# Fourteen products whose sum nobody reads, behind the sums of five norms of a two-model kernel

## The reference, cut to what matters

```python
def rms_norm(x, g):
    xf = x.astype(jnp.float32)
    y = xf * lax.rsqrt(jnp.mean(xf * xf, axis=-1, keepdims=True) + EPS)
    return (y * g.astype(jnp.float32)).astype(x.dtype)

for l in range(DEPTH):                                   # DEPTH = 2
    ...
    h = rms_norm(x, norm1_g[l]) * (1.0 + sc1) + sh1
    proj = h @ w_in[l]
    ...
    x = x + g1 * mixed
    h = rms_norm(x, norm2_g[l]) * (1.0 + sc2) + sh2
    u = causal_dwconv(h @ w_up[l], ffn_conv_w[l], ffn_conv_b[l])
    ...
    x = x + g2 * ((jax.nn.silu(gate) * val) @ w_down[l])

# second block, once
hn = rms_norm_2(x, norm_g);  proj = hn @ w_in            # then attention of three kinds, y @ w_out
hn = rms_norm_2(x, norm_g);  x + jnp.square(jax.nn.relu(hn @ w_up)) @ w_down
```

## Time and profile before

| | |
|---|---|
| median of three runs | 1836.68 us (1833.19 to 1836.99) |
| profiled execution, its own time | 1837.2 us |
| its span, first to last instruction | 1835.6 us |
| PE busy | 1691.9 us (92%) |
| POOL busy | 1255.8 us (68%) |
| DVE, ACT busy | 872.4 us (48%), 861.5 us (47%) |
| share of the last-ended chain on PE | 76% |
| mean granted clock of PE | 0.935 of full |

### The profile page before, as it was taken

One profiled execution on the slowest core, in us unless ns is written; L12 is line 12 of the kernel. 1 busy time (PEld: TensorE's weight loads), 2 busy tenths in 40 slices (PEclk: granted clock), 3 DMA queues, 4 the chain that ended last, 5 costly groups with the idle time before them and its releaser, 6 DMA issues.

```text
span 1835.6 us, 33961 instructions
## 1 busy us (share of the span) xinstructions
PE 1691.9 (92%) x13290; PEld 1639.6 (89%) x13290; DVE 872.4 (48%) x1774; ACT 861.5 (47%) x1411; POOL 1255.8 (68%) x948
## 2 busy tenths in 40 slices
PE   8999998989989999899998989979999986579999
PEld 8998997989889999899997989879999984479999
DVE  2457576466445643567665475434431354532200
ACT  2254444554346653464454554346654442335532
POOL 1467965656569999567965656658988790048886
PEclk8699999989889999999998989989999896589999
DMA  7245753446436667446753557446656650035664
GB/s 271 85 150 165 247 181 121 162 160 219 137 128 210 229 200 250 122 145 184 253 167 121 162 176 232 121 122 178 184 173 186 212 171 15 1 92 172 184 184 128
DMA packets 85518, 302.75 MB, mean 165 GB/s; under 512 B 9840, under 2 KB 12528, under 8 KB 85104
## 3 DMA queue, kind: packets, MB, share of 16 engines
q1 hardware_dynamic: 85360, 300.59, 51.2%
HBM read 299.50 MB, written 1.05 MB: 164 GB/s over the span
## 4 chain that ended last, share of the span: by engine, by line
PE 76%; DVE 10%; POOL 4%; issue 3%; ACT 3%; DVEq 2%; DMA 1%; SPq 0%; ACTq 0%; POOLq 0%
PE gemm_bank L1441 62%; POOL w_lo L390 4%; PE turn_bank L1548 2%; PE turn_bank L1518 1%; PE score_bank L1518 1%; ACT w_hi L408 1%; PE outp_bank L1536 1%; DVE rstd_row L766 1%; DVE conv L746 1%; PE outp_bank L1695 1%; DMA ada_w<-in_w_ada 1%; DVE idx_score L746 1%; PE score_bank L1441 1%; PE outp_bank L1583 1%; DVE probs L933 1%
## 5 line engine op out<-in xcount | busy, mean ns | idle before, releaser
L390 POOL TENSOR_TENSOR w_lo<-w_raw,w_hi 128x512 fp32r<-128x512 f32 x944 | 1255.6, 1358 | 568.3 <-ACT w_hi L408 566.3
L408 ACT ACTIVATE w_hi<-w_raw 128x1024 fp32r<-128x1024 f32 x472 | 492.6, 1046 | 700.5 <-PE gemm_bank L1441 673.2
L1441 PE MATMUL gemm_bank<-h_hi,w_hi 128*128 128x256 f32 x2112 | 613.6, 291 | 41.4 <-DVE h_lo L746 16.2
L1441 PE MATMUL gemm_bank<-h_lo,w_hi 128*128 128x256 f32 x2112 | 604.9, 286 | 0.0
L1441 PE MATMUL gemm_bank<-h_hi,w_lo 128*128 128x256 f32 x2112 | 604.6, 286 | 0.0
L1441 PEld LDWEIGHTS gemm_bank<-h_hi,w_hi 128*128 128x128 f32 x2112 | 412.9, 196 | 52.3 <-DVE h_lo L746 17.0
L1441 PEld LDWEIGHTS gemm_bank<-h_lo,w_hi 128*128 128x128 f32 x2112 | 413.2, 196 | 0.1
L1441 PEld LDWEIGHTS gemm_bank<-h_hi,w_lo 128*128 128x128 f32 x2112 | 412.7, 195 | 0.0
L746 DVE SCALAR_TENSOR_TENSOR conv<-gemm_bank,params_sb,conv 128x255 f32<-128x255 f32 (+1 forms) x320 | 139.5, 477 | 186.6 <-ACT conv L681 130.5
L1441 PE MATMUL gemm_bank<-w_hi,h_hi 128*128 128x256 f32 (+2 forms) x704 | 207.8, 295 | 18.4 <-DVE h_lo L746 8.0
L1441 PE MATMUL gemm_bank<-w_lo,h_hi 128*128 128x256 f32 (+2 forms) x704 | 202.7, 288 | 0.0
(11 more groups left out here) (284 smaller groups left out, 2268.9 us busy)
## 6 DMA issues: line engine op xcount, KB each, us to landing
w_raw<-in_stream SPq DMA_DIRECT2D x458, 512.0 KB, 3.7
ada_w<-in_w_ada SPq DMA_DIRECT2D x80, 512.0 KB, 4.8
ada_first<-in_w_ada SPq DMA_DIRECT2D x16, 512.0 KB, 10.6
w_raw<-in_stream SPq DMA_DIRECT2D x8, 256.0 KB, 2.7
alibi_sb<-in_alibi SPq DMA_DIRECT2D x1, 1920.0 KB, 7.3
rows_sb<-in_rows SPq DMA_DIRECT2D x1, 1536.0 KB, 10.6
residual<-in_x_t SPq DMA_DIRECT2D x1, 1024.0 KB, 7.4
out_x<-residual SPq DMA_DIRECT2D x4, 256.0 KB, 4.4
```

Of the source, the lines that this page charges most:

```text
L390: ins = nc.gpsimd.tensor_tensor(w_lo[:, s, e], w_raw[:, s, e], w_hi[:, s, e].bitcast(f32), ALU.subtract)
L408: A(w_hi[:, s, 0:n], w_raw[:, s, 0:n], ACT.Copy).then_inc(hi_ready, 1)
L1441: ins = M(o, a, b, start=first and i == 0, stop=last and i == len(passes) - 1, skip_group_check=True)
```

## The change

A function `filler` is added to PE's program. It multiplies the ones with the first 256 columns of the constants 14 times, each time into the same columns of `S.bank[0]`, and nothing reads them. square_sum_x calls it behind its own products, after the semaphore increment that releases DVE, in every norm but the first. Nothing else changes, on PE or on any other engine.

```diff
+            def filler():
+                for i in range(14):
+                    M(S.bank[0][:, 0:SEQ], ones[:, 0:P], cst[:, 0:SEQ], start=True, stop=True)
+
             def square_sum_x(l, which):
                 i = (O_N2 if which else O_N1) if l < DEPTH else (O2_N2 if which else O2_N1)
                 b, out = take(O, l, i)
...
                         pe.wait_ge(sq_ready, (2 * l + which) * 4 + kt // 2 + 1)
                     ins = M(out[:, 0:SEQ], ones[:, 0:P], sq[:, kt, :], start=kt == 0, stop=kt == KT - 1)
                 ins.then_inc(o_full, 1)
+                if l or which:
+                    filler()
```

## The result

The changed kernel took 1824.11 us (median of seven runs, 1816.74 to 1828.25), and the kernel before 1833.19 us in its seven runs (1827.9 to 1837.8; the three shown ahead of the prediction are among them). The ratio is 0.9945, with a 95% interval of 0.9925 to 0.9966. On the 1836.68 us from which the forecast counted, that is 10.1 us (6.2 to 13.8) less. I had forecast 5.5.

What follows compares the result with a forecast made beforehand. PE was taken to bound the kernel, by standing idle and by working at half clock. Of 10.8 us behind five norms, falls take 5.3, leaving 5.5: 1836.68 - 5.5 = 1831.2 us, range 1825.5 to 1835.0.

Steps and rivals of the forecast that it cites:

- What the half clock cost: Behind the five norms' waits for h, PE works at 0.50 for 24.21 us; at most 10.8 us can be won.
- The length of the filler, 6.1 us, and its cover: In the five norms' waits for h, 28 passes take 6.1 us and leave 2.0 or 1.7 us of idle time.
- Whether what lies behind keeps pace: Behind the norms' restarts, weights and h arrive in time for faster products; loss 0, bound 1 us in all.
- The price of a fall, 1.5 us: Behind a shortened wait at a norm, losing the clock costs 1.5 us, against 2.2 us on average now.
- The number of falls, 3.5 of five: At the five norms' shortened waits, the clock falls in 3.5, which takes 5.3 us from the gain.
- seven idle times: PE idle times of 1.51 to 2.75 us in the trace, begun at full clock; five were followed by half clock.
- The advice of the Trainium skill: Rival at the norms: shortened waits are harmless, the clock holds, 10.8 us won, 1825.9 us; chance 0.25.

## Why the prediction was wrong

- **What the half clock cost, 10.8 us.** Right. With 17 products the same stretches held 90 products more, 10.9 us, and the time fell by 12.8 us (8.4 to 17.1).
- **The length of the filler, 6.1 us, and its cover.** Right. It ended 6.0 us behind the sums, the idle time left was 2.05, 1.97, 2.05, 1.74 and 1.75 us, and the restart didn't move.
- **Whether what lies behind keeps pace.** Right at the norms: 48 products took 5.85 us at four restarts.
- **The price of a fall, 1.5 us.** Right: 36 products instead of 48.
- **The number of falls, 3.5 of five.** This is the step that failed. It was 4 of 15. The sum with 1.3 falls is 10.8 - 2.0 = 8.8 us, within the interval of what was measured. I had pooled seven idle times because their lengths were near, and had taken the share of falls among them for a chance that holds at any wait. The runs show no such chance. Longer idle times lost the clock more often behind the filler (none of 30 restarts with 0.4 to 0.8 us, 4 of 15 with 1.73 to 2.05, 4 of 5 with 2.60 to 2.91), but elsewhere the idle time of 1.51 us in the first two layers' attention was followed by half clock in 13 of 28 cases, and that of 2.35 to 2.40 us for the convolution in 18 of 28, counted over the profiles of all runs here. At one place and one length the cases sort themselves by another quantity, how long before the idle time the clock had last risen:

| idle time, between the same two instructions | clock had last risen | what followed |
|---|---|---|
| 1.51 us, attention | 59.9 to 60.8 us ahead | held in 15 of 15 |
| 1.51 us, attention | 58.7 to 59.6 us ahead | fell in 9 of 9 |
| 2.35 to 2.40 us, convolution | 74.0 to 74.5 us ahead | held in 5 of 5 |
| 2.35 to 2.40 us, convolution | 74.8 to 75.9 us ahead | fell in 14 of 14 |

The other 13 cases had risen at quite other times. Two cases of the attention in the second layer, each with its 1.51 us and then the 3.5 us behind it, first with 7 products in the norms (last risen 60.2 us ahead), then with the one-column products (59.6 us ahead):

```profile
1140.34 0.43 PE L1589 MATMUL outp_bank<-qkv,probsT 128*128 128x64 f32 x2 [1.51 <-DVE probsT L906]
1140.34:1143.84 3.50, 3.25 (x27) 3.01 (x28) 1.36 (x4) 1.44 (x2) 0.73 (x1) 1.00 0.02 5
```

```profile
1144.17 0.45 PE L1589 MATMUL outp_bank<-qkv,probsT 128*128 128x64 f32 x2 [1.51 <-DVE probsT L906]
1144.17:1147.67 3.50, 3.50 (x17) 3.16 (x17) 1.37 (x4) 1.43 (x2) 0.01 (x1) 0.54 0.01 4
```

So at one place and one length the outcome goes with the moment, and less than a microsecond lies between the moments that held and those that fell. What stands around an idle time may count as well, but that isn't shown. An idle time of 2.04 to 2.08 us ahead of a product on bc_conv lost the clock in ten of ten, and one of 2.05 us behind the filler in none of six; yet the clock had last risen 82.4 to 82.9 or 351.9 to 358.9 us ahead in the ten, and 56.7 to 63.9 us ahead in the six.

One of the ten, in the changed kernel's own profile:

```profile
830.96 0.67 PE L1645 MATMUL score_bank<-bc_conv 128*128 128x256 f32 x2 [2.07 <-DVE c_dot_b L1101]
```

```profile
830.96:835.22 4.26, 4.26 (x22) 4.21 (x23) 3.92 (x13) 0.52 (x1) 1.67 (x2) 0.60 0.69 218
```

- **The advice of the Trainium skill.** The Trainium skill, "TensorE: Matmul & The Clock Gate", section "Why this matters for your kernels", advises to leave no idle gaps of more than about 3 us between bursts of products. I weighed it against seven rows and gave its time a chance of 0.25. It was nearer than my forecast for this filler: its 1825.9 us lies 0.7 us from what the ratio gives for 1836.68 us, 1826.6. As a rule it doesn't hold here: the clock was lost behind idle times of 1.75 and 1.96 us of this filler, and 12 products left 2.6 to 2.9 us and lost it in four of five.
- **The median that I counted from.** 1836.68 us was of three runs; seven have 1833.19. By the ratio alone the changed kernel would stand at 1826.6 us, inside the range of 1825.5 to 1835.0. Its median of 1824.11 is outside because the kernel before moved by 3.5 us as well. The range should have taken in the spread of the runs on both sides.

In all three profiles of 14 products the clock fell at norm (2, second), 1.45 to 1.51 us behind the restart. The length alone isn't the reason: norm (2, first) had the same idle time, 1.73 to 1.74 us against 1.75 to 1.76, and held in all three. The three falls are hardly three separate cases, since the clock had last risen 32.6 to 32.7 us ahead of that restart in each; 12 products, with 32.6 us too, lost it there as well. The length does count at that moment: with 17 products and 0.46 or 0.47 us of idle time, three kernels whose clock had risen 32.1 to 33.0 us ahead held it. So 4 of 15 is a count and no rate for other kernels, and that four of five norms held in the first profile is in part luck of the moment.

What stays open is what stretch of the past decides the clock, and whether sparser neighbours of an idle time make a fall likelier.

## What to carry to other kernels

Look at the granted clock in the first microseconds behind each long wait of TensorE, and price it as the products that start there against as many at full clock. Products that nobody reads kept it up in 30 of 30 waits here when they had 256 columns, left 0.4 to 0.8 us of the wait, and ended before it did; half as many won nothing, and those that overran were paid for the most part. One profile doesn't give the chance of a fall, since the same wait goes either way with the moment. And a clock that is up more isn't time won: in the third layer a mean of 0.96 for 0.90 brought nothing where other engines set the pace. Loops in which TensorE is idle a little in each turn are worth a look first: here the half clock lasted in one, and two products a turn were worth as much as all the norms.

## What the runs showed of the hardware

- 56 one-column passes with full weight loads kept PE busy in the profile for all of 8.98 us, and the clock went to 0.50 in them. The busy time shows them like work.
- At a clock of 0.50 throughout, a loop with PE busy for 22.72 of 27.47 us did not get the full clock back. With four passes of 256 columns more in each turn it ran at 1.00.
- The same program in two executions differed by 7.1 us over its first 535 us, at mean clocks of 0.93 and 0.95.
- One idle time of 1.51 us, between the same two instructions, kept the full clock in 15 cases and was followed by half clock in 13. Where the clock had last risen 58.7 to 60.8 us ahead of it, the 9 cases up to 59.6 us fell and the 15 from 59.9 us on held.
